# A two-layer hybrid network on one core: waits, late constants, an index list and the order at the end

## The reference, cut to what matters

```
for l in range(2):
    sh1, sc1, g1, sh2, sc2, g2 = split(silu(c) @ ada_w[l] + ada_b[l], 6)        # the same for c_ctx
    a = modulate(rmsnorm(h, norm1_w[l]), sh1, sc1)
    out = ssd_mixer(a) if l == 0 else attn_mixer(a)      # ssd: projection, conv of 5 taps, chunked scan both ways
    h = h + g1 * out
    m = modulate(rmsnorm(h, norm2_w[l]), sh2, sc2)
    h = h + g2 * grouped_moe(m)      # 1 shared expert + 2 of 16 experts for each token, chosen inside 1 of 4 groups
return rmsnorm(h, final_norm_w)                          # layer 1 only needs the latent tokens: 256 instead of 512
```

## Time and profile before

| what | value |
|---|---|
| median of three timed runs | 1557.12 us |
| the profiled execution, its own time | 1554.12 us |
| its span from first to last instruction | 1552.2 us |
| PE busy | 1416.5 us (91%) |
| DVE, ACT, GpSimd busy | 529.4, 385.9, 188.6 us |
| moved by DMA | 334.46 MB |
| mean granted TensorE clock | 0.966 |

### The profile page before, as it was taken

The page is one execution under the profiler, slowest core; times in us unless marked ns, Lnnn a source line. Parts: engine busy times, 40 slices in busy tenths (PEclk is TensorE's granted clock), DMA queues, the critical chain, the costliest instruction groups (busy, mean ns, idle before and its releaser), DMA issues.

```text
span 1552.2 us, 28858 instructions
## 1 busy us (share of the span) xinstructions
PE 1416.5 (91%) x12332; PEld 810.3 (52%) x12332; DVE 529.4 (34%) x954; ACT 385.9 (25%) x949; POOL 188.6 (12%) x213
## 2 busy tenths in 40 slices
PE   5999889999988999979999998998999989999884
PEld 2543445455545544435556655654756766655442
DVE  2544655545443221144122211115255351222112
ACT  2311334233333320030122221213044211222111
POOL 0000134224142210000011111000000001111100
PEclk9799999999999999989999999999999999999987
DMA  9364434344332352102999999994330349999993
GB/s 369 112 201 154 136 109 142 103 136 139 133 109 82 82 135 81 54 4 86 404 405 390 382 382 383 393 330 161 122 109 1 125 159 371 395 397 399 401 405 139
DMA packets 130260, 334.46 MB, mean 215 GB/s; under 512 B 13203, under 2 KB 63051, under 8 KB 123979
## 3 DMA queue, kind: packets, MB, share of 16 engines
q1 hardware_dynamic: 117739, 308.02, 54.3%
q0 software_dynamic: 6144, 12.60, 2.3%
q10 hardware_dynamic: 6240, 11.90, 2.1%
HBM read 325.65 MB, written 14.68 MB: 219 GB/s over the span
## 4 chain that ended last, share of the span: by engine, by line
PE 69%; SPq 15%; DMA 7%; DVE 4%; ACT 2%; issue 2%; DVEq 0%; POOLq 0%; ACTq 0%
SPq L547 11%; PE ps L1159 11%; PE ps L1467 8%; PE ps L1176 7%; PE ps L1371 7%; PE ps L1421 4%; PE ps L1506 4%; SPq L549 3%; PE ps L1102 3%; PE ps L1264 2%; PE ps L1765 2%; PE ps L1531 2%; PE ps L1677 2%; DMA tmp<-in_ada_w 2%; PE ps L1251 2%
## 5 line engine op out<-in xcount | busy, mean ns | idle before, releaser
L1159 PE MATMUL ps<-aT,ring 128*128 128x512 f32 x384 | 175.7, 607 | 0.0
L1467 PE MATMUL ps<-ring,ssb 128*32 128x256 f32 x2224 | 134.5, 383 | 5.8 <-DMA ring<-in_moe_w_up 4.1
L2179 DVE COPY big<-ps 32x256 f32<-32x256 f32 x160 | 67.7, 423 | 146.9 <-PE ps L1506 145.2
L1159 PEld LDWEIGHTS ps<-aT,ring 128*128 128x128 f32 x384 | 71.9, 194 | 84.3 <-issue 84.3
L1176 PE MATMUL ps<-aT,ring 128*128 128x512 f32 x256 | 114.2, 595 | 0.0
L1371 PE MATMUL ps<-big,ring 128*128 128x512 f32 x256 | 110.2, 592 | 0.0
L1467 PEld LDWEIGHTS ps<-ring,ssb 128*32 128x32 f32 x2224 | 82.2, 111 | 51.7 <-DMA ring<-in_moe_w_up 8.0
L2170 DVE TENSOR_TENSOR ssb<-ssb,ps 128x256 f32<-128x256 f32 (+1 forms) x53 | 18.6, 355 | 256.1 <-ACT ssb L960 256.1
L1467 PE MATMUL ps<-tmp,ssb 128*32 128x256 f32 x1728 | 100.2, 379 | 4.0 <-DMA tmp<-in_moe_w_up 4.0
L867 ACT ACTIVATE ssb<-ps,ncum 128x128 f32<-128x128 f32 x256 | 73.1, 371 | 97.2 <-PE ps L1239 96.4
L1421 PE MATMUL ps<-aT,ring 128*128 128x512 f32 (+1 forms) x256 | 87.9, 500 | 6.8 <-ACT aT L795 6.8
(11 more groups left out here) (388 smaller groups left out, 1860.7 us busy)
## 6 DMA issues: line engine op xcount, KB each, us to landing
ring<-in_ada_w SPq DMA_DIRECT2D x44, 1024.0 KB
ring<-in_moe_w_down SPq DMA_DIRECT2D x40, 1024.0 KB
ring<-in_moe_w_gate SPq DMA_DIRECT2D x56, 512.0 KB
ring<-in_moe_w_up SPq DMA_DIRECT2D x56, 512.0 KB
tmp<-in_moe_w_gate SPq DMA_DIRECT2D x48, 512.0 KB
tmp<-in_moe_w_up SPq DMA_DIRECT2D x48, 512.0 KB
ring<-in_ssd_in_w SPq DMA_DIRECT2D x20, 1024.0 KB
tmp<-in_moe_w_down SPq DMA_DIRECT2D x16, 1024.0 KB
```

The costliest lines, as they stand in the source:

```text
L1159: ins = pe.matmul(ps[:, bank, :], slot(u)[:, k, (i % 2) * P:(i % 2 + 1) * P], aT[:, k, :], start=(k == 0), stop=(k == KD - 1))
L1467: ins = pe.matmul(tiled_gu[32 * c:32 * c + 32, 2 * h + i, :].rearrange("p (r n) -> p r n", r=2), XgT[l][:, k * C + 32 * g:k * C + 32 * g + ...
L2179: ins = dve.tensor_copy(Y[s % 2][32 * g:32 * g + 32, 256 * c:256 * c + 256], tiled_y[32 * c:32 * c + 32, 2 * h + i, :])
```

## The change

- `take_state`: for all but the first states DVE multiplies ahead of the wait for the state's bank, and waits only before the add.
- Late constants: SP loads only the 128 x 128 identity out of `c32` at the start (64 KB). ACT issues the other 448 KB and `c16` after the first norm's modulation. PE waits for them before the cumulative sums (i = 6). ACT's first chunks wait for nine counts of `s_set` instead of ten.
- Bank 3: `turn_b(0)` moves from i = 9 to i = 8, ahead of `ada_turn(1)`, and ACT's copy with it.
- Gather: GpSimd waits for `gidx` alone. SP issues the first load of the chosen experts in either layer only after both index lists are there.
- `halves`: in layer 1, steps with 64 rows up to step 8 (steps 3, 5 and 7) go in two halves.
- End of layer 1: the quarters of steps 13 and 15 are computed after the last expert. The rows are read back as two 512 KB pieces for the first 128 tokens, then 1 MB for the others.

```diff
 def halves(l, s):
-    return [list(range(G))] if G <= 1 + l else [...]
+    return [list(range(G))] if G <= 1 + (l and s > 8) else [...]
 def bank3_uses(n):
-        return [("ada", 0), ("ada", 1), ("BK", 0)] + [("TR", c) for c in range(8, 13)]
+        return [("ada", 0), ("BK", 0), ("ada", 1)] + [("TR", c) for c in range(8, 13)]
-        shared_at = [10, 12, 13, 15]
+        shared_at = [10, 12]
-            sp_.dma_start(c32[:, :], a["c32"]).then_inc(s_x, 16)
+            sp_.dma_start(ident, a["c32"][:, 0:P]).then_inc(s_x, 16)
...
                     if u.slot in held:
                         sp_.wait_ge(*held[u.slot])
-                    else:
-                        sp_.wait_ge(s_gi, 3)
+                    if s == AHEAD_EXPERTS[l] and j == 0 or u.slot not in held:
+                        sp_.wait_ge(s_gi, 3 * l + 3)
...
-            pool.wait_ge(s_const, 16 * (n_consts + 1))
+            pool.wait_ge(s_const, 16 * (n_consts + 2))
...
-                    pool.wait_ge(s_gi, 3 * l + 3)
+                    pool.wait_ge(s_gi, 3 * l + 2)
...
-                if i == 0:
-                    act.dma_start(c16f, a["c16"]).then_inc(s_const, 16)
                 act.wait_ge(s_ms, i + 1)
...
                     ins.then_inc(s_a, 1)
+                if i == 0:
+                    act.dma_start(c32[:, P:], a["c32"][:, P:]).then_inc(s_const, 16)
+                    act.dma_start(c16f, a["c16"]).then_inc(s_const, 16)
-                    act.wait_ge(s_set, 10)
+                    act.wait_ge(s_set, 9)
-                if i == 10:
+                if i == 9:
                     take_b(0)
...
-                    for t in range(nt - l):
-                        act.dma_start(ypair[:, t, :, :], pairs[:, t, :, :]).then_inc(s_yp[l][t], 16)
                     if l:
                         for c in range(2):
-                            act.dma_start(ypair[:, 1, :, c * 512:(c + 1) * 512], pairs[:, 1, :, ...])
+                            act.dma_start(ypair[:, 0, :, c * 512:(c + 1) * 512], pairs[:, 0, :, ...])
+                        act.dma_start(ypair[:, 1, :, :], pairs[:, 1, :, :]).then_inc(s_yp[1][2], 16)
+                    else:
+                        for t in range(nt):
+                            act.dma_start(ypair[:, t, :, :], pairs[:, t, :, :]).then_inc(s_yp[0][t], 16)
...
                 if i == 6:
+                    pe.wait_ge(s_const, 16 * (n_consts + 2))
                     pe.wait_ge(s_sp, 6)
...
+                if i == 8:
+                    turn_b(0)
                 if i == 9:
                     ada_turn(1)
-                    turn_b(0)
...
                     if l:
+                        for i in range(len(shared_at), 4):
+                            shared_tokens(i)
                         pe.wait_ge(s_acc[l], 4)
                         for i in range(4):
-                            pe.wait_ge(s_yp[l][max(0, i - 1)], 16)
+                            pe.wait_ge(s_yp[l][min(i, 2)], 16)
                             add_pairs(i)
...
-                dve.wait_ge(s_b4, B4["st", g, q] + 1)
                 if n == 0:
+                    dve.wait_ge(s_b4, B4["st", g, q] + 1)
                     dve.tensor_copy(H[d][0], ps[:, 4, :]).then_inc(s_b4v, 1)
                 else:
                     dve.wait_ge(s_b4v, B4["st", g, q - 2] + 1)
                     link(dve.tensor_tensor(per_head(H[d][n]), per_head(H[d][n - 1]),
                                            heads(cdec[:, t, :], d * NH + g * HG), ALU.mult))
+                    dve.wait_ge(s_b4, B4["st", g, q] + 1)
                     dve.tensor_tensor(H[d][n], H[d][n], ps[:, 4, :], ALU.add).then_inc(s_b4v, 1)
```

More of the change, by code:

```diff
@@ L88, in halves @@
     G = step_rows(l, s) // 32
-    return [list(range(G))] if G <= 1 + l else [list(range((G + 1) // 2)), list(range((G + 1) // 2, G))]
+    return [list(range(G))] if G <= 1 + (l and s > 8) else [list(range((G + 1) // 2)), list(range((G + 1) // 2, G))]
 def halves_to(l, s):
@@ L1010, in moe_act @@
                     pairs = y_rows[l].rearrange("(k t p) n -> p t k n", k=2, p=P)
-                    for t in range(nt - l):
-                        act.dma_start(ypair[:, t, :, :], pairs[:, t, :, :]).then_inc(s_yp[l][t], 16)
                     if l:
                         for c in range(2):
-                            act.dma_start(ypair[:, 1, :, c * 512:(c + 1) * 512], pairs[:, 1, :, c * 512:(c + 1) * 512])\
-                                .then_inc(s_yp[1][1 + c], 16)
+                            act.dma_start(ypair[:, 0, :, c * 512:(c + 1) * 512], pairs[:, 0, :, c * 512:(c + 1) * 512])\
+                                .then_inc(s_yp[1][c], 16)
+                        act.dma_start(ypair[:, 1, :, :], pairs[:, 1, :, :]).then_inc(s_yp[1][2], 16)
+                    else:
+                        for t in range(nt):
+                            act.dma_start(ypair[:, t, :, :], pairs[:, t, :, :]).then_inc(s_yp[0][t], 16)
                 with act.Else():
@@ L1604, in moe_pe @@
                                 pe.wait_ge(s_sdw, 16 * KF)
-                            if s == NE - 1:
-                                pe.wait_ge(s_xd[l], NE)
                             shared_tokens(shared_at.index(s))
```

## The result

The changed kernel takes 1545.18 us (median of four runs, 1544.32 to 1546.60), the kernel before 1557.47 us beside it (1556.64 to 1559.11, four runs); the ratio is 0.9921, with a 95% interval of 0.9903 to 0.9938. 1543.4 us was forecast. The profiled execution took 1545.94 us (span 1544.2), 8.2 less than the one of before.

The account below looks back on a forecast made before the run. Bytes bound the start and both expert stages, PE the stages between. Terms -2.4 - 5.1 - 6.8 - 2.0 + 3.4 + 1.5 - 2.3 = -13.7 took 1554.1 to 1540.4, plus 3.0: 1543.4 us; 8-in-10 range 1533 to 1552.

Parts of the forecast that it names:

- Late constants: Start: fewer bytes ahead of the first weight units, 2.4 us less; bounds 0 to 3.2 less.
- turn_b: Turn of B ahead of ada_turn(1): PE's idle time and the slower next chunk go, 5.1 us less; bounds 3.1 to 5.7.
- Early multiply and clock: Scan: multiplying ahead of the bank's wait gives 6.8 us less, and 2.0 by the clock; bounds 4.5 to 10.6.
- Gate in layer 0: Experts of layer 0: SP's whole weight stream waits for the lists, 3.4 us more.
- Rival B: Expert streams: slot releases, not bytes, pace them; gates cost nothing, PE's 5.2 us come through, 1533.3 us; chance 0.10.
- Gate in layer 1: Experts of layer 1: DMA work begins 1.6 us later, 1.5 us more; nothing booked for PE's earlier rows.
- The end: End of layer 1: late quarters and a smaller first read-back, less step 15's lost filler, 2.3 us less.
- Rival A: Start: PE's clock stays warm, 6.6 us less, total 1536.8 us; chance 0.12.
- C: Rival, turn and scan: another producer is late once the named one is early, total 1549.7 us; chance 0.15.
- D: Rival, end of layer 1: without fillers PE's clock stays low from step 13, total 1559.7 us; chance 0.04.
- Halves: Layer 1, steps 3, 5, 7: waits of 0.85 us each saved in a byte-bound stage, 0; bounds 2.6 less, 1 more.

Follow-up runs that it names:

- the second profile: The kernel before, unchanged, profiled again: 1559.88 us, 5.8 more than its first profile.

## Why the prediction was right, step by step

- **Late constants: wrong, even in sign.** "2.4 us less" came out as 1.4 more in the first pair of profiles and 2.8 by the medians. The step divided the bytes taken away by 369 GB/s, as if the queue stayed full. It didn't: in 10 to 13 us the engines idled and the bytes' time was lost again. What made a loss of it was the mean square, later and in most profiles partly at the lower clock. The part about `c16` is right in direction, and its size is about 0.4. The lower bound ("if other bytes fill the gap it is 0") excluded a loss without a reason.
- **turn_b: right.** 5.1 forecast, 5.5 in the trace, 6.0 when undone.
- **Early multiply and clock: the mechanism right, the size too small.** 8.8 forecast. The scan got 10.5 us shorter (11.6 against the second profile), and undoing it costs 12 to 13. The waits gave a little less than was summed: 14.0 us to 7.2, but GpSimd's late product in step 11, foreseen at 0.5, takes back 1.1, so 5.7 for 6.8. The clock was booked at half of what two stretches cost; the changed kernel also stays up at 510 to 520 us (0.84 in the first profile of before). The Trainium skill, TensorE: Matmul & The Clock Gate, Part 1, says that the default state is throttled and activity releases it. The trace agrees, with some 7 us at the lower level for 27 when the waits are long, and that is what was sized too small: 2.0 booked, where 4.8 to 7.5 us of the scan's difference are left when the waits are taken off.
- **Gate in layer 0: 3.4 forecast, 4.3 measured.** Without the gate the next unit goes out at 722.93, 5.6 us behind the first load at 717.36, where it was 3.9 in the kernel before: there was more to lose than I had read off. The 3.9 was that one profile's: in the second profile of before it is 5.6 too. Rival B is out: the stream's end moved with its beginning.
- **Gate in layer 1: 1.5 forecast, 1.0 to 1.3 in the stages, 1.5 and 2.4 by medians,** each with overlapping runs. PE's 5.3 us of waiting shrank to 2.80, without worth, as booked.
- **The end: 2.3 forecast, 2 in most profiles, by another sum.** From the last `w_up` to the end of the span are 32.6 and 33.1 us in the two profiles of before, and 30.2 to 31.0 in ten of the twelve with the change. The two others are the changed kernel itself (32.8) and the one with the old pieces (32.9), both with pairs of 8.82 us. The quarters bring nothing: in their old places the end is as short (30.7). The small piece lands about 0.6 us sooner where 1.3 were booked, and that can keep the clock up through the pairs. All three profiles with the old order of the pieces are at 32.6 to 33.1, ten of the eleven with the new one at 30.2 to 31.0. That points to the pieces as the source of these 2 us; with one profile of the edit by itself, and medians 1.8 apart with overlapping runs, it is likely and not shown.
- **Rival A: out.** L1149 took its 13.89 us at the lower clock everywhere. **C** came true in one wait of 1.1 us. **D**: the clock did fall in step 15, and rose again as the two quarters began.
- **Halves** were not tested. They lie in the stretch from layer 1's flag to the last `w_up`, which is as long as before, but the gate lies there too.

The total is nearer than its terms. The steps summed to 13.7 us less; the spans of the two first profiles differ by 8.0. Measured stage by stage in that pair, the start was 3.8 too good, layer 0's experts 2.4, and layer 1's experts with the end 1.3; turn and scan gave 1.8 more than booked. Layer 0's 2.4 holds something that no step had. One block of 32 matmuls (L1426, at 702 us) ran partly at the lower clock and took 15.68 us where it had taken 13.98, and the lists, and with them the gate, came 1.3 us later behind it. The other way, I added 3.0 us because the first profile of before was a quick execution, but that of the changed kernel was none (0.8 above its median). By the medians the change gave 12.3 us, and against the second profile of before 13.9. So 1.8 us of error in the total is partly luck: errors of nearly 4 us stood in both directions, one in the step for the start and one in the choice of the profile.

## What to carry to other kernels

In a two-operand update whose one operand waits for another engine, do the half that needs only old data ahead of the wait; where the waits come close together, count the clock too, which here was worth about as much as the waits. A gate that keeps a stream of weights back for a small gather is paid for when the stage is bound by bytes (4.3 us for a delay of 5.6 in layer 0), and what it bought here was worth nothing. Bytes removed from the head of a load queue aren't time removed: look whether the engines stay full behind them. And where stages vary by 1 to 3 us between executions, read a stage of 5 us in several profiles before you call an edit without effect.

## What the hardware showed that I had not expected

- Taking 448 KB from the first load of SP's queue made the issue of a later pair of 1 MB loads take 2.62 us for 0.94, with the DMA engines at 0.47 to 0.70 from 10 to 13 us; all eight profiled starts with the split show such a hole there, 2 to 3 us long, and none of the six with the whole load does.
- Half the bytes saved far less than half the time: PE had the first read-back 4.3 to 4.5 us after its issue in nine of eleven profiles when it was 512 KB, and 5.0 to 5.1 us in three of three when it was 1 MB, each with other pieces issued right behind it.
- With waits of 0.4 to 1.6 us ahead of them, the four pair sums took 7.4 to 7.8 us (nine profiles); with waits of 2.07 and 2.21 us the clock fell among them and they took 8.8 (two profiles).
- One kernel without any change gave 1549.9 to 1563.3 us in 25 runs, and the difference between two of its profiles lies in no one stage.
